# Placing the rows of expert blocks in another order of partitions, and passing over the empty ones

## What is computed

```python
def routed_experts(xt, idx, gate, w_exp_gu, w_exp_down):
    # token-slots sorted by expert, each expert's rows padded to whole blocks of 128 rows
    def run_block(args):
        tok, g, e = args
        return swiglu(x_pad[tok], w_exp_gu[e], w_exp_down[e]) * g[:, None]
    out = lax.map(run_block, (row_tok.reshape(n_blocks, MOE_BLOCK),
                              row_gate.reshape(n_blocks, MOE_BLOCK), block_expert))
    return jnp.zeros((T + 1, D), xt.dtype).at[row_tok].add(out.reshape(R, D))[:T]

def moe(...):
    ...
    routed = routed_experts(xt, idx, gate.astype(x.dtype), w_exp_gu, w_exp_down)
    shared = swiglu(xt, w_sh_gu, w_sh_down)
    return (routed + shared).reshape(B, L, D)
```

## Time and profile before

| | us |
|---|---|
| median of 3 runs | 2080.55 (2080.55 to 2083.68) |
| the profiled execution | 2079.63 |
| its span in the trace | 2077.8 |
| PE busy | 1959.6 (94%) |
| DVE busy | 929.9 (45%) |
| POOL busy | 618.8 (30%) |
| ACT busy | 562.7 (27%) |
| mean granted clock of TensorE | 0.981 of full speed |

### The profile page before, as it was taken

How to read it: one execution, slowest core, us unless ns; L and a number is a source line. 1 busy time by engine, 2 the same in 40 slices (tenths; PEclk the granted TensorE clock), 3 DMA queues, 4 the chain that set the end, 5 groups by cost and what they waited for, 6 DMA issues and landing times.

```text
span 2077.8 us, 23451 instructions
## 1 busy us (share of the span) xinstructions
PE 1959.6 (94%) x7658; PEld 1084.7 (52%) x7658; DVE 929.9 (45%) x2467; ACT 562.7 (27%) x1147; POOL 618.8 (30%) x792
## 2 busy tenths in 40 slices
PE   8998999999999999999999899999999999999990
PEld 6786645666555665556555463444444444444440
DVE  4374465999765533030344743233332332332324
ACT  2223554562566640030233000111111111111114
POOL 0042000101220001101223254545445555555444
PEclk9999999999999999999999999999999999999995
DMA  6031212110110011134211406999999999999995
GB/s 189 3 38 14 64 41 102 41 47 5 26 26 3 1 31 48 44 132 126 103 61 48 155 31 217 376 369 373 381 373 375 378 373 376 375 373 377 375 364 193
DMA packets 130467, 365.09 MB, mean 176 GB/s; under 512 B 34641, under 2 KB 82514, under 8 KB 112594
## 3 DMA queue, kind: packets, MB, share of 16 engines
q1 hardware_dynamic: 105250, 289.80, 37.2%
q0 software_dynamic: 23328, 72.90, 13.6%
q10 hardware_dynamic: 1808, 1.33, 0.2%
HBM read 310.82 MB, written 53.04 MB: 175 GB/s over the span
## 4 chain that ended last, share of the span: by engine, by line
PE 55%; DMA 19%; DVE 8%; issue 7%; POOL 7%; ACT 2%; POOLq 0%; SPq 0%; DVEq 0%; ACTq 0%
DMA arena<-x_d,tid 17%; PE psum L630 11%; PE psum L774 9%; PE psum L792 6%; PE psum L645 4%; POOL arena L1293 3%; PE psum L845 3%; PE psum L444 3%; POOL acc_d L1287 2%; PE psum L479 2%; PE psum L708 2%; ACT arena L1341 2%; DVE arena L2264 2%; DMA acc_d<-arena,sid 2%; PE psum L491 2%
## 5 line engine op out<-in xcount | busy, mean ns | idle before, releaser
L1341 ACT ACTIVATE arena<-psum 128x512 f32<-128x512 f32 (+8 forms) x643 | 286.0, 486 | 1086.6 <-PE psum L918 429.7
L918 PE MATMUL psum<-arena 128*128 128x512 f32 x1088 | 484.3, 598 | 27.8 <-DVE arena L2264 24.9
L918 PEld LDWEIGHTS psum<-arena 128*128 128x128 f32 x1088 | 201.6, 190 | 267.2 <-issue 265.0
L1293 POOL DMA_INDIRECT arena<-x_d,tid x276 | 264.9, 960 | 85.8 <-issue 71.3
L932 PE MATMUL psum<-arena 128*128 128x512 f32 x544 | 244.7, 593 | 0.5 <-ACT arena L1341 0.5
L630 PE MATMUL psum<-arena 128*128 128x384 f32 (+1 forms) x768 | 239.7, 471 | 0.2 <-DMA arena<-in_w_glu 0.2
L2314 DVE TENSOR_TENSOR arena<-arena,psum 128x256 f32<-128x256 f32 x68 | 28.6, 421 | 457.7 <-ACT arena L1341 457.7
L630 PEld LDWEIGHTS psum<-arena 128*128 128x128 f32 x768 | 144.5, 190 | 94.7 <-issue 10.9
L774 PE MATMUL psum<-arena 128*128 128x384 f32 (+1 forms) x576 | 177.7, 472 | 1.1 <-DVE arena L2075 1.1
L2264 DVE STREAM_TRANSPOSE arena<-arena 128x256 f32<-128x256 f32 x272 | 150.3, 610 | 54.7 <-DMA arena<-x_d,tid 53.7
L932 PEld LDWEIGHTS psum<-arena 128*128 128x128 f32 x544 | 103.5, 190 | 130.0 <-issue 129.4
(11 more groups left out here) (313 smaller groups left out, 2148.1 us busy)
## 6 DMA issues: line engine op xcount, KB each, us to landing
arena<-in_w_exp_gu SPq DMA_DIRECT2D x69, 2048.0 KB, 10.4
arena<-in_w_exp_down SPq DMA_DIRECT2D x68, 1024.0 KB, 10.8
arena<-in_w_in SPq DMA_DIRECT2D x24, 512.0 KB, 4.5
arena<-in_x_prompt SPq DMA_DIRECT2D x10, 512.0 KB, 4.2
arena<-x_d,tid POOLq DMA_INDIRECT x276, 8.8
arena<-in_w_glu SPq DMA_DIRECT2D x16, 256.0 KB, 4.9
arena<-in_w_attn_proj SPq DMA_DIRECT2D x16, 256.0 KB, 4.5
arena<-in_w_out SPq DMA_DIRECT2D x1, 4096.0 KB, 14.4
```

Of the source, the lines that this page charges most:

```text
L918: last = mm(psum[:, 2, :], xgT[u][:, k, :], ewg[u][:, k, :], start=k == 0, stop=k == DK - 1)
L1293: pool.indirect_dma_start(xg[u][:, g, :], None, x1_d.rearrange("t (a f) -> (t a) f", a=4), bass.IndirectOffsetOnAxis(ap=tid[u][:, g:g + 1] ...
L1341: return act.activation(dst, src, fn, **kw)
```

## The change

It has three parts. First, the place of a row within its block is compared with a tile `place` that holds, for partition p = 16a + 8b + c (a from 0 to 7, b 0 or 1, c from 0 to 7), the number (17a + 8b + 16c) mod 128, in place of p itself. Each number from 0 to 127 occurs once. A block with n rows fills numbers 0 to n-1, so its 128-n empty places no longer are the last partitions: every run of 8 neighbouring partitions (one a and b) holds numbers 16 apart, and with n rows about n/16 of its 8 places are filled. POOL makes the tile with one `iota` ahead of its wait for the slots, and two DVE instructions with their waits take it modulo 128 after `block_and_place`. Second, the gathers and scatters are told a highest valid row, and that a row above it is no error; the empty places' rows lie above it. Third, `gate_shared(2)` is moved from between the first five and the last four `slots` to ahead of all of them.

```diff
+        place, wrapped = at(47616, P), at(47616 + P, P)
...
+            pool.iota(place.rearrange("p (a b c) -> p a b c", a=8, b=2), [[17, 8], [8, 2], [16, 8]], base=0,
+                      channel_multiplier=0, allow_small_or_imprecise_dtypes=True).then_inc(s("constants"), 1)
+
             pool.wait_ge(s("slots_ready"), 1)
...
             def scatter(u, rows_):
                 pool.indirect_dma_start(acc_d, bass.IndirectOffsetOnAxis(ap=sid[u][:, 0:1], axis=0), rows_, None,
+                                        bounds_check=T - 1, oob_is_err=False,
                                         compute_op=ALU.add).then_inc(s(f"y_stored{u}"), 16)
 
             def gather(u):
                 for g in range(4):
                     pool.indirect_dma_start(xg[u][:, g, :], None, x1_d.rearrange("t (a f) -> (t a) f", a=4),
-                                            bass.IndirectOffsetOnAxis(ap=tid[u][:, g:g + 1], axis=0)
-                                            ).then_inc(s(f"xg_loaded{u}"), 16)
+                                            bass.IndirectOffsetOnAxis(ap=tid[u][:, g:g + 1], axis=0),
+                                            bounds_check=4 * T - 1, oob_is_err=False).then_inc(s(f"xg_loaded{u}"), 16)
...
                 dve.wait_ge(s("slots_ready"), 1)
+                dve.wait_ge(s("constants"), 11)
+                step(ts(wrapped, place, P - 0.5, -float(P), ALU.is_ge, ALU.mult))
+                step(tt(place, place, wrapped, ALU.add))
...
             gate_shared(1)
             dve.wait_ge(s("x1_stored"), 16 * NT)
+            gate_shared(2)
             for i in range(NT + 1):
-                if 2 <= i + 1 < NT and i > 0:
+                if 3 <= i + 1 < NT:
                     gate_shared(i + 1)
...
-                    ts(o[:, 0:P], iota64[0:r, :], sin_[0:r, m // MK, k:k + 1], None, ALU.is_equal)
+                    ts(o[:, 0:P], place[0:r, :], sin_[0:r, m // MK, k:k + 1], None, ALU.is_equal)
```

## The result

The changed kernel takes 2071.19 us (median of 5 runs, 2068.94 to 2073.08), the kernel before 2081.61 (2080.55 to 2083.68). The ratio is 0.9947 with a 95% interval of 0.9933 to 0.9962: faster by half a per cent, where 2039.5 us and two per cent had been forecast. The profiled execution took 2068.95 us with a span of 2067.1, 10.7 less than before.

What follows compares the result with a forecast made beforehand. DMA was taken to bound the loop at 11.17 us a block, PE next at 10.55. Gains of 34 (loop), 5.5 (its end) and 1.2 (gate product), 41 us in all, took 2079.63 to 2038.9, stated as 2039.5, range 2030 to 2058.

Steps and rivals of the forecast that it cites:

- What bounds the loop: Expert loop: DMA sets the distance of 11.17 us a block, while PE alone could go at 10.55.
- Order of partitions: Gathers and scatters: order alone gains nothing; with 8 neighbouring partitions to an engine, each loses its share in every block.
- uneven engines: Rival for the expert loop: some engine's share stays full in nearly every block; 10.84 us a block, 2051.5 us, chance 0.23.
- Empty places passed over: Expert loop: 25% of gathered and scattered rows go, giving 10.65 us a block, 34 us gained, bounds 24 and 41.
- what the prediction named last, a scatter whose landing hardly shortens: Expert loop: named as what would make the prediction wrong, holding the distance near 11 us with engines idle.
- The sign the prediction named for this rival: Changed profile under uneven engines: bytes down by a fourth, distance 10.8 us or more, DMA share well below 1.
- Bytes: POOL's queue in the middle of the loop: down by a fourth, to 7.0 MB per 9 blocks.
- End of the loop: Last scatters and the result's load: last two scatters land 3.4 us after their start; 5.5 us gained, bounds 0 and 6.
- The check on POOL: Indirect instructions on POOL: checking rows taken as zero cost; up to 4.1 us a block would be covered.
- The third gate product: Planning stage: PE's 9.5 us stall goes, 8 come back waiting for POOL's tokens; 1.2 us gained, bounds 0 and 2.

Runs made afterwards that it cites:

- run 4: Changed kernel with the rows at every fourth partition left out in every block and all other places moved, empty ones too: 2038.77 us.
- Run 1: Changed kernel with another order: each group of partitions 0 to 3 and 32 to 35, and so on, gets places 16 apart; 2046.01 us, ratio 0.9824 to kernel before.
- run 7: Changed kernel with places 6 and 7 of every eight left out in every block and all others moved, empty ones too: 2143.45 us.
- run 9: As run 4, every fourth place left out, except that places 3 and 35 are kept, so 30 of 128 are left out: 2088.94 us.
- run 6: Changed kernel leaving out, in every block, the 32 places its order leaves empty in a block of 96 rows, all others moved: 2080.05 us.
- run 8: As run 4, but only the scatter passes over every fourth place; the gathers bring all 128 rows: 2042.21 us.
- run 10: As run 4, but only the gathers pass over every fourth place; the scatter adds all 128 rows: 2063.28 us.
- run 5: Changed kernel with places 96 to 127 of every block left out and all others moved, empty ones too: 2115.91 us.
- run 2: Changed kernel with rows in their own order of partitions as before the change, empty places still passed over: 2079.89 us, ratio 0.999 to the kernel before.
- run 3: Changed kernel with its order and moved gate product, but without the check of the rows, so no row is passed over: 2079.35 us.
- Run 12: Changed kernel with its order and the check, but the highest valid row set so high that all 128 rows are moved: 2082.12 us.

## Why the prediction was wrong

**What bounds the loop** was right: PE's 10.55 and the DMA's 11.17. An even sparing reaches PE's floor (run 4).

**The step that failed is "Order of partitions".** It took an engine to have 8 neighbouring partitions, and so counted the 0.99 us of an average engine for every engine. No row of the trace before had shown which engine takes a partition. The shown rival, uneven engines, was the true case, and 0.23 was too little for it. Runs 1, 7 and 9 show the sharing: even by fours 32 apart gains, even by eights loses, and places 3 and 35 act as one engine's. By the order of the change the numbers of partitions 0 to 3 are 0, 16, 32, 48 and those of 32 to 35 are 34, 50, 66, 82, so that engine's scatter is full in any block of over 82 rows. The sizes of POOL's packets in the trace bear out the fours for the gathers: in run 4 all 8832 packets of the gathers have 3076 bytes, three pieces of 1 KB and a remnant, and in run 7 half of them have 4096 and half, 4416, have 2056. The Trainium skill, "DMA: Bandwidth & Descriptors", section "The descriptor swizzle", says for a plain transfer that an engine takes four partitions and the four 32 further on. These runs agree with it for indirect gathers and scatters.

**"Empty places passed over"** holds once the engines are even. Run 1's loop is 707.83 us, 29.4 less than before, where 34 had been forecast with bounds 24 and 41.

**The rival's size was off too.** It gave 10.84 us a block, as the full engine's own sum: full scatter, three quarters of the gathers. Measured were 11.18, and 11.20 with the pattern fixed (run 6). The step that failed there is "a block's weights, gathers and scatter are only there when the slowest engine is done", taken as if the slowest engine then took no more than its sum. With equal engines sums hold within 0.15 us (runs 8, 10). With unequal ones the excess over the sum is 0.36 us (run 6), 0.34 (run 9), 0.9 (run 5) and 1.05 (run 7), steady, of which the check is 0.06 at most.

What the excess is made of stays open. Three things are seen, and no run separates them. First, pauses as in run 7, where PE waits longer for the gathered rows and SP orders new weights only after PE; the changed kernel has the excess without such a trough. Second, longer packets: SP's queue, with the same bytes, took 773 us of all 16 engines before and 794 in the changed kernel, 814 in run 5 and 820 in run 7, but also 782 in run 4, where the load is even. Third, the chain of scatters on POOL, each of which starts only when the one before it has landed. From issue to landing (from 1400 to 2000 us, the kernel before, the changed kernel, runs 1, 4 and 9; then POOL's wait for it in the changed kernel and in run 4):

```profile
acc_d<-arena,sid POOLq DMA_INDIRECT x54, 10.8
...
acc_d<-arena,sid POOLq DMA_INDIRECT x54, 10.3
...
acc_d<-arena,sid POOLq DMA_INDIRECT x56, 9.3
...
acc_d<-arena,sid POOLq DMA_INDIRECT x57, 8.8
...
acc_d<-arena,sid POOLq DMA_INDIRECT x53, 10.7
```
```profile
POOL carry L1307 <- DMA acc_d<-arena,sid: 180.8, 50, 6.2
...
POOL carry L1310 <- DMA acc_d<-arena,sid: 22.8, 5, 8.7
```

A landing of 10.3 or 10.7 us and the 0.7 us from the landing to the next scatter are 11.0 and 11.4, nearly the distances of 11.18 and 11.35. The kernel before has 10.8 and 0.3. Run 4 waits for it in 5 blocks only. So what the prediction named last, a scatter whose landing hardly shortens, came true. Whether the landing sets the pace or is late because the engines are full isn't shown: no run let a scatter start before the last had landed, gave SP a third buffer, or released the weights earlier. Run 12 shows only that 0.4 us more in this chain add 0.06 when all rows are moved.

**The sign the prediction named for this rival,** a DMA share well below 1, didn't show in the changed kernel (1.01), only in runs 5 (0.96) and 7 (0.92). The packets' time has grown in its place: 21 us of q1. Read the GB/s beside the share: 354 against 375.

**Bytes** were right over the whole kernel, 54.60 / 72.90, a quarter less. The 7.72 MB from 1500 to 1600 us are more than the 7.0 forecast for such a stretch, as the blocks worked there hold more than the mean of 96 rows.

**End of the loop** was right in size, 5.6 us against 5.5 forecast, with some luck: the landing took 2.8 us where 3.4 had been taken, and the last scatter started 1.0 us after its rows were ready where 0.4 had been. It waited until the scatter of 8 rows had landed (2025.93), 0.3 us after the rows, and then for the check.

**The check on POOL** was right in what it does to the time: 0.6 us a block in place of none, within its cover of 4.1.

**The third gate product** had the mechanism right and the size off: 0.5 us against 1.2. POOL took 0.83 us a token tile here (20 in 16.63 us), 15.0 us for 18 and not 14.6, and behind the last the product's two instructions and the change to `shared_down` take 0.8 us more, where the sum had 0.4. The stall of 9.5 us did go, and came back as a wait for POOL.

**First ten steps.** The prediction spread the gain over all 66. In the kernel before the first three, in the changed kernel and in runs 2 and 3 the first four are at PE's 10.5 to 10.6 while the queues fill. The changed kernel keeps this up for ten (105.72 / 10), with blocks of 12 and 61 rows among them (counted from the small packets of each scatter in the trace).

## What to carry to other kernels

Before leaving rows out of a transfer, ask which DMA engine carries them: a transfer is as late as its fullest engine, and an uneven one can cost more than moving everything (a quarter fewer rows gave 2039 us, 2080, 2116 or 2143 by nothing but their places, against 2082 with every row moved). Where the loads are uneven, compare a measured distance with the same work spread evenly, and not with the fullest engine's sum. And a stall that a freed buffer ends is worth only the distance to the next producer, here POOL's tokens.

## What the runs showed of the hardware that was not expected

- A row that a scatter passes over still has a packet, a small one; a gather's packets, of four pieces each, get shorter. POOL's queue has 23328 packets with 72.90 MB and with 54.60, and in run 4 the packets under 512 bytes grow by 2176, which is 68 scatters times 32 rows and nothing for the gathers. The page's line before, and in run 4:

```profile
DMA packets 130467, 365.09 MB, mean 176 GB/s; under 512 B 34641, under 2 KB 82514, under 8 KB 112594
...
DMA packets 130467, 347.18 MB, mean 170 GB/s; under 512 B 36817, under 2 KB 84690, under 8 KB 112594
```

- Two kept rows of 32 cost 0.80 us a block (runs 4 and 9), as they fill one engine's scatter.
- Passing rows over lengthens the packets of another queue with the same 289.80 MB, and more so with unequal loads: q1 took 773 us of all 16 engines before, 782 in run 4 (even), 794 in the changed kernel and 820 in run 7.
- The check of the rows costs POOL 0.39 us ahead of a scatter and 0.05 us in each gather.
